# Experts with more than 64 rows: passes of 128 rows on the full array in place of passes of 64 rows, with one turn of the semaphores per expert

## The reference, cut to what matters

```python
hg = jnp.einsum('td,edf->tef', h, w_gate)      # h: 384 tokens x 1024
hu = jnp.einsum('td,edf->tef', h, w_up)        # w_gate, w_up: 16 x 1024 x 512
act = jax.nn.silu(hg) * hu * gates[..., None]
return jnp.einsum('tef,efd->td', act, w_down)  # w_down: 16 x 512 x 1024
```

## Time and profile before

| | |
|---|---|
| median of 3 runs | 616.38 us (616.27 to 617.57) |
| profiled execution | 621.26 us, span 619.4 us |
| PE busy | 492.6 us (80% of the span) |
| DVE, ACT, POOL busy | 224.1, 142.8, 86.1 us |
| bytes moved by DMA | 164.52 MB, mean 266 GB/s |
| `gate_up` instructions on PE (L676) | 672, 165.2 us |
| `down` instructions on PE (L689) | 336, 75.8 us |

### The profile page before, as it was taken

The page is one execution under the profiler, slowest core; times in us unless marked ns, Lnnn a source line. Parts: engine busy times, 40 slices in busy tenths (PEclk is TensorE's granted clock), DMA queues, the critical chain, the costliest instruction groups (busy, mean ns, idle before and its releaser), DMA issues.

```text
span 619.4 us, 7520 instructions
## 1 busy us (share of the span) xinstructions
PE 492.6 (80%) x2624; PEld 234.0 (38%) x2625; DVE 224.1 (36%) x616; ACT 142.8 (23%) x263; POOL 86.1 (14%) x177
## 2 busy tenths in 40 slices
PE   1769889999989999950479899999988878788800
PEld 1225688544478544630243233333332222222200
DVE  3589855999982105560020010110110010101027
ACT  3555842601148201300030010110110010100023
POOL 2000603888000151013000000000000000000030
PEclk9998989999989999975589999999998797978965
DMA  8980340733994931049648993879999999996162
GB/s 296 366 329 0 120 136 6 286 136 120 388 387 183 378 147 43 26 159 392 263 168 335 391 379 108 353 301 411 431 424 423 423 423 422 423 423 266 35 215 107
DMA packets 38032, 164.52 MB, mean 266 GB/s; under 512 B 2776, under 2 KB 3544, under 8 KB 32240
## 3 DMA queue, kind: packets, MB, share of 16 engines
q1 hardware_dynamic: 31120, 145.79, 59.9%
q10 hardware_dynamic: 4608, 10.86, 4.8%
q0 software_dynamic: 2272, 7.46, 3.4%
HBM read 152.76 MB, written 11.34 MB: 265 GB/s over the span
## 4 chain that ended last, share of the span: by engine, by line
issue 51%; PE 30%; DVE 7%; DMA 5%; ACT 4%; POOL 1%; ACTq 0%; POOLq 0%; DVEq 0%
PE psum L604 7%; PE psum L487 3%; PE psum L553 3%; PE psum L479 3%; DMA arena<-in_x_sample 3%; PE psum L509 3%; PE psum L578 3%; PE psum L418 2%; DMA arena<-in_w_mod 2%; PE psum L598 2%; PE psum L628 1%; ACT arena L802 1%; POOL sorted_tokens L1519 1%; DMA arena<-sorted_outputs,pos_u 1%; PE psum L496 1%
## 5 line engine op out<-in xcount | busy, mean ns | idle before, releaser
L676 PE MATMUL psum<-arena 128*64 128x512 f32 x672 | 165.2, 648 | 31.5 <-DMA arena<-in_w_up 21.2
L676 PEld LDWEIGHTS psum<-arena 128*64 128x64 f32 x672 | 51.9, 148 | 131.2 <-issue 111.6
L689 PE MATMUL psum<-arena 128*64 128x512 f32 x336 | 75.8, 592 | 2.3 <-ACTq L972 2.3
L1364 DVE TENSOR_TENSOR arena<-arena,psum 128x256 f32<-128x256 f32 x21 | 8.9, 422 | 183.4 <-ACT arena L956 183.4
L1527 POOL DMA_INDIRECT arena<-sorted_outputs,pos_u x6 | 5.7, 952 | 308.6 <-DMA sorted_outputs<-arena 307.1
L689 PEld LDWEIGHTS psum<-arena 128*64 128x64 f32 x336 | 25.1, 137 | 48.8 <-issue 48.8
L956 ACT ACTIVATE arena<-psum 128x256 f32<-128x256 f32 x21 | 8.1, 384 | 146.2 <-PE psum L676 130.7
L604 PE MATMUL psum<-arena 128*128 128x512 f32 x96 | 41.5, 592 | 0.0
L418 PE MATMUL psum<-arena 128*2 128x256 f32 x256 | 30.7, 395 | 0.3 <-DMA arena<-in_w_mod 0.3
L660 PE MATMUL psum<-arena 128*128 128x128 f32 x48 | 6.7, 302 | 27.0 <-DMA arena<-sorted_tokens 27.0
L961 ACT ACTIVATE arena<-psum 128x512 f32<-128x512 f32 x21 | 12.5, 597 | 66.7 <-PE psum L689 66.7
(11 more groups left out here) (278 smaller groups left out, 586.2 us busy)
## 6 DMA issues: line engine op xcount, KB each, us to landing
arena<-in_w_gate SPq DMA_DIRECT2D x16, 2048.0 KB, 17.5
arena<-in_w_up SPq DMA_DIRECT2D x16, 2048.0 KB, 22.3
arena<-in_w_down SPq DMA_DIRECT2D x16, 2048.0 KB, 19.8
arena<-in_w_mod SPq DMA_DIRECT2D x12, 2048.0 KB, 13.8
arena<-in_w_in SPq DMA_DIRECT2D x3, 2048.0 KB, 19.1
sorted_outputs<-arena ACTq DMA_DIRECT2D x42, 128.0 KB, 6.5
arena<-in_w_out SPq DMA_DIRECT2D x2, 2048.0 KB, 17.5
arena<-modulation_rows ACTq DMA_DIRECT2D x3, 1024.0 KB, 11.2
```

Source lines behind the costliest of these rows:

```text
L676: last = mm(bank[0][HALF * t:HALF * t + HALF, :], xs[:, k, :], gu[:, :, k, t * 256:t * 256 + 256], start=(k == 0), stop=(k == KD - 1))
L689: last = mm(bank[4][HALF * h:HALF * h + HALF, :], hiddenT[:, s * P + t * HALF:s * P + t * HALF + HALF], dn[:, 2 * t + s, h * 512:h * 512 + ...
```

## The change

- An expert of up to 64 rows is computed as before, in one pass (`gate_up_narrow`, `down_narrow`).
- An expert of more than 64 rows has a first pass of 128 rows on the full array: 16 matmuls of 128 columns by 512 for gate and up, each into a PSUM bank of its own (`gate_up_wide`), four transposes, 8 matmuls for down (`down_wide`). Silu, product and copies are twice as wide, the stores 256 KB each.
- Rows beyond 128 go into one or two extra passes of 128 rows with semaphores of their own (`extra_product`, `extra_scalar`, `extra_vector`). In an extra pass every step waits for the one before, and the next expert's first pass begins behind it with nothing beside it.
- The semaphores of the first pass move once per expert: `gated` and `downed` by 2, the others by 1. `skipped` is gone, and `n` is read again at the head of `first_pass`, behind the waits for `xs` and the weights.
- Buffers move within the arena: `xs` and `hidden` are twice as large, silu writes to `hidden`, two staging buffers of 1024 take the place of three of 512. One block of 128 padding rows instead of two.

With the given counts, experts 0, 3 and 15 take one wide pass each, expert 2 a wide pass and a wide extra pass, and the other twelve one narrow pass each.

```diff
-SORTED = PAIRS + 2 * P
+SORTED = PAIRS + P
 SETS = 3
-PASSES = 6
+PASSES = 3
...
-        xs = view(F + 11264, KD, HALF)
-        hiddenT = view(F + 11776, 256)
-        sg = view(F + 12032, 256)
-        hidden = view(F + 12288, 256)
-        ystage = view(F + 12544, 3, 512)
+        xs = view(F + 10240, KD, P)
+        hidden = view(F + 11264, 512)
+        hiddenT = view(F + 11776, 512)
+        ystage = view(F + 12288, 2, D)
...
-        def turn(p, e):
-            return e * PASSES + p
+        def extra(e, q, step, steps):
+            return e * (2 * steps) + (q * steps + step)
+        def all_written(e, q):
+            return e * (32 * PASSES) + (32 * q + 32)
...
-                sp.wait_ge(S("gated"), (e - 2) * PASSES)
+                sp.wait_ge(S("gated"), 2 * (e - 2))
                 load_gate_up(j, e)
-                sp.wait_ge(S("downed"), (e - 2) * PASSES + 1)
+                sp.wait_ge(S("downed"), 2 * (e - 2))
...
+            def gate_up_wide(j, sem):
                 gu = expert_weights(j)[0]
-                pe.wait_ge(S("x_staged"), at + 1)
-                if fresh is not None:
-                    pe.wait_ge(S(f"gu_in{j}"), fresh * 32)
+                for k in range(KD):
+                    for h in range(2):
+                        last = mm(bank[h][:, :], xs[:, k, :], gu[:, h, k, :], start=(k == 0), stop=(k == KD - 1))
+                last.then_inc(S(sem), 1)
+            def gate_up_narrow(j):
+                gu = expert_weights(j)[0]
                 for k in range(KD):
                     for t in range(2):
-                        last = mm(bank[0][HALF * t:HALF * t + HALF, :], xs[:, k, :],
+                        last = mm(bank[0][HALF * t:HALF * t + HALF, :], xs[:, k, 0:HALF],
                                   gu[:, :, k, t * 256:t * 256 + 256], start=(k == 0), stop=(k == KD - 1))
-                last.then_inc(S("gated"), 1)
-            def down(j, fresh, turned, evacuated):
+                last.then_inc(S("gated"), 2)
...
+            def down_wide(j, sem, inc):
                 dn = expert_weights(j)[1]
-                pe.wait_ge(S(f"dn_in{j}"), fresh * 16)
-                pe.wait_ge(S("evacuated"), evacuated + 1)
-                pe.wait_ge(S("turned"), turned + 1)
+                for c in range(4):
+                    for h in range(2):
+                        last = mm(bank[4 + h][:, :], hiddenT[:, c * P:c * P + P], dn[:, c, h * 512:h * 512 + 512],
+                                  start=(c == 0), stop=(c == 3))
+                last.then_inc(S(sem), inc)
...
-            def skipped(e, done):
-                pe.wait_ge(S("gated"), turn(done, e))
-                pe.wait_ge(S("crossed"), turn(done, e))
-                pe.wait_ge(S("downed"), turn(done, e))
-                pe.sem_inc(S("gated"), PASSES - done)
-                pe.sem_inc(S("crossed"), PASSES - done)
-                pe.sem_inc(S("downed"), PASSES - done)
...
+            def first_pass(j, e, fresh, between):
+                pe.wait_ge(S("x_staged"), e + 1)
+                pe.wait_ge(S(f"gu_in{j}"), fresh * 32)
                 n = pe.value_load(n_i[0:1, bass.ds(e, 1)], min_val=0, max_val=NT * P)
                 with pe.If(n > HALF):
-                    gate_up(j, turn(1, e), None)
-                    down(j, use + 1, turn(1, e), turn(0, e))
-                    transposes(turn(1, e))
-                    with pe.If(n > P):
-                        gate_up(j, turn(2, e), None)
-                        down(j, use + 1, turn(2, e), turn(1, e))
-                        transposes(turn(2, e))
-                        with pe.If(n > P + HALF):
-                            with pe.Fori(3, PASSES) as q:
-                                gate_up(j, q + turn(0, e), None)
-                                down(j, use + 1, q + turn(0, e), q + turn(0, e) + -1)
-                                transposes(q + turn(0, e))
-                        with pe.Else():
-                            skipped(e, 3)
+                    gate_up_wide(j, "gated")
+                    between()
+                    pe.wait_ge(S("multiplied"), e + 1)
+                    transposes(4, "crossed")
+                with pe.Else():
+                    gate_up_narrow(j)
+                    between()
+                    pe.wait_ge(S("multiplied"), e + 1)
+                    transposes(2, "crossed")
+            def extra_pass(j, e, q):
+                pe.wait_ge(S("extra_vector"), extra(e, q, 1, 3))
+                gate_up_wide(j, "extra_product")
+                pe.wait_ge(S("extra_vector"), extra(e, q, 2, 3))
+                transposes(4, "extra_product")
+                pe.wait_ge(S("extra_vector"), extra(e, q, 3, 3))
+                if q == 0:
+                    pe.wait_ge(S("evacuated"), e + 2)
+                else:
+                    pe.wait_ge(S("extra_scalar"), extra(e, 0, 2, 2))
+                down_wide(j, "extra_product", 1)
+            def extra_passes(j, e, m):
+                extra_pass(j, e, 0)
+                with pe.If(m > 2 * P):
+                    extra_pass(j, e, 1)
+                with pe.Else():
+                    pe.wait_ge(S("extra_scalar"), extra(e, 0, 2, 2))
+                    pe.sem_inc(S("extra_product"), 3)
+            def expert(j, e, use):
+                nothing = lambda: None
+                m = pe.value_load(n_i[0:1, bass.ds(e, 1)], min_val=0, max_val=NT * P)
+                following = ((j + 1) % SETS, e + 1, use + (j + 1) // SETS + 1)
+                with pe.If(m > HALF):
+                    with pe.If(m > P):
+                        down(j, e, use + 1, True, 1)
+                        extra_passes(j, e, m)
+                        pe.wait_ge(S("extra_product"), extra(e, 2, 0, 3))
+                        pe.sem_inc(S("gated"), 1)
+                        pe.sem_inc(S("downed"), 1)
+                        pe.wait_ge(S("extra_scalar"), extra(e, 2, 0, 2))
+                        first_pass(*following, nothing)
                     with pe.Else():
-                        skipped(e, 2)
+                        pe.sem_inc(S("gated"), 1)
+                        pe.sem_inc(S("extra_product"), 6)
+                        first_pass(*following, lambda: down(j, e, use + 1, True, 2))
...
+                    first_pass(*following, lambda: down(j, e, use + 1, False, 2))
...
+            def extra_pass(e, q, y):
+                row = first_row(e, P * (q + 1))
+                act.wait_ge(S("extra_product"), extra(e, q, 1, 3))
+                A(hidden[:, :], bank[0][:, :], ACT.Silu).then_inc(S("extra_scalar"), 1)
+                act.wait_ge(S("extra_product"), extra(e, q, 3, 3))
+                A(ystage[:, y, :], psum[:, 4:6, :].rearrange("p a b -> p (a b)"), ACT.Copy
+                  ).then_inc(S("extra_scalar"), 1)
+                act.wait_ge(S("extra_scalar"), extra(e, q, 2, 2))
+                act.wait_ge(S("written"), all_written(e, q + 1))
+                store_wide(row + P * (q + 1), y)
+            def extra_passes(e, y, m):
+                extra_pass(e, 0, 1 - y)
+                with act.If(m > 2 * P):
+                    extra_pass(e, 1, y)
+                with act.Else():
+                    act.wait_ge(S("extra_product"), extra(e, 2, 0, 3))
+                    act.sem_inc(S("extra_scalar"), 2)
+                    act.sem_inc(S("written"), 32)
+            def no_extra():
+                act.sem_inc(S("extra_scalar"), 4)
+                act.sem_inc(S("written"), 64)
...
+                with act.If(m > HALF):
+                    with act.If(m > P):
+                        evacuate_wide(e, y)
+                        extra_passes(e, y, m)
+                        act.wait_ge(S("written"), all_written(e, 3))
+                        gate(e + 1)
...
+            def multiply_wide(sem):
+                tt(hidden[:, :], hidden[:, :], bank[1][:, :], ALU.mult).then_inc(S(sem), 1)
...
+            def expert(e):
+                m = dve.value_load(n_i[0:1, bass.ds(e, 1)], min_val=0, max_val=NT * P)
+                nxt = dve.value_load(off_i[0:1, bass.ds(e + 1, 1)], min_val=0, max_val=PAIRS)
+                with dve.If(m > P):
+                    main_turn(e)
+                    extra_passes(e, m)
+                    stage_x(nxt, "x_staged")
+                with dve.Else():
+                    dve.sem_inc(S("extra_vector"), 6)
+                    stage_x(nxt, "x_staged")
+                    main_turn(e)
+                multiply(e + 1)
```

More of the change, by code:

```diff
@@ L711, in expert_rest, with transposes, down @@
-            def expert_rest(j, e, use):
+                last.then_inc(S("downed"), 2)
+            def transposes(n, sem):
+                for c in range(n):
+                    last = tr(bank[2][:, c * P:c * P + P], hidden[:, c * P:c * P + P], ident[:, :])
+                last.then_inc(S(sem), 1)
+            def down(j, e, fresh, wide, inc):
+                pe.wait_ge(S(f"dn_in{j}"), fresh * 16)
+                pe.wait_ge(S("evacuated"), e + 1)
```

(58 more changed lines are left out.)

178 lines of the change are left out of this document (66 added, 112 removed).

## The result

The changed kernel takes 716.5 us (median of four runs, 708.0 to 720.0) against 616.3 us: a ratio of 1.158, interval 1.151 to 1.164. I had forecast 638 us, in a range of 631 to 645. The direction was right and the size was wrong by 78 us.

What follows compares the result with a forecast made beforehand. The prediction took the weight stream, started by expert 3's last `down`, as the bound. A shift of 21.5 us, plus 0.6 for stores, less 0.3 in the tail, gave 21.8 on the median of 616.4: 638.2 us, range 631 to 645.

Steps and rivals of the forecast that it cites:

- the code loading: Rival: PE stops 1.19 us for code at turns of experts 1 to 4 and within the extra pass; 644 us, chance 0.12.
- What bounds the kernel before: The weight stream sets the end, 15.4 us per expert; its start depends on PE finishing expert 3's last `down`.
- the decisive point: End of expert 3's last `down`, 415.9 us before; said to move expert 15's weights one for one.
- the stores: Expert 3's rows stored once, behind the point: 0.26 MB more in the stream, 0.6 us.
- A wide pass costs two narrow ones: On PE, wide `gate_up` 13.8 us against 13.84 for two narrow; wide `down` 6.9 against 2 x 3.46.
- Expert 2's extra 10.3 us: Expert 2 pays two wide passes, 41.4 us, for three narrow ones, 31.1: 10.3 us more ahead of the point.
- The open steps: Extra pass: silu and product exposed before the transposes, 1.4 us, and the copy before `down`, 0.8 us.
- the turn to expert 3: After expert 2's extra pass PE waits for ACT's copies and stores, 3.0 us, plus 0.6 for the row-count load.
- The sum without reloading: PE's steps with no code reloads, through the weight stream and tail to the kernel's end: 638.2 us.
- The forecast shift of 21.5 us: Delay of expert 3's last `down`: 17.5 us from the steps plus 4.0 from slow clock starts.
- The clock: Slow starts after waits: 2.5 us at expert 3's `gate_up`, 1.5 at expert 4's, 4.0 together; bounds 0 and 9.
- The tail: From the arrival of expert 15's weights to the end of the kernel: 0.3 us less than before.

Runs made afterwards that it cites:

- compact: The changed kernel with PE's code for an expert written once, branches choosing only a step's matmuls; loop body 91 KB; 647.3 us, 1.051 to before.
- compact_short_one: compact with a narrow extra pass for at most 64 remaining rows and without PE's code for rows beyond 256; 636.2 us, 1.028 to before.
- pad157: The kernel before with 104 matmuls per expert that never run in the innermost branch; loop body 157 KB; 672.7 us, 1.088 to before.
- noweights: The changed kernel without the weight loads of experts 3 to 15, SP only setting their semaphores; 692.1 us, 1.121 to before.
- pad100: The kernel before with 28 matmuls per expert that never run in the innermost branch; loop body 100 KB; 654.6 us, 1.064 to before.
- nosecond: The changed kernel without PE's code for the second extra pass, which no expert runs; loop body 137 KB; 732.9 us, 1.186 to before.

## Why the prediction was wrong, point by point

**The step that failed** is the code loading. The sum put it at nothing, and the rival, with a chance of 0.12, had its price and its reach wrong: "5 x 1.19 = 6 more: 644. Later turns are covered by the stream." A stop costs not 1.19 but 9.5 to 14.0 us at eight of the turns, with two to six code packets in each; what I took for the price, the 1.19 us at 350.25, came behind one packet at 347.9 and may be only the visible end of its load. And the loads come back on every turn of the loop, up to the last experts, where PE has only 3.7 us to spare against the weights (15.4 less 11.7); so PE becomes the bound and the stream gets holes. Written once, the same steps took 69 us less. The page of before had the number that would have warned: 19 code packets, all of PE's code once. I did not set the 157 KB of the new loop beside the 79 KB of the old one.

**What bounds the kernel before** was right: in compact, which is bound by the weights again, expert 15 starts 29.5 us later where the decisive point moved by 27.8 and the stores were put at 0.6.

**A wide pass costs two narrow ones**: right. 13.9 and 7.1 us were measured, 13.8 and 6.9 forecast.

**Expert 2's extra 10.3 us**: right, 11.1 by the medians of compact and compact_short_one, 10.0 by their traces.

**The open steps**: right. 1.41 and 0.86 us against 1.4 and 0.8; the turn to expert 3 3.92 against 3.6.

**The sum without reloading** was too low as well: 638.2 against the compact form's 647.3, which lies outside my range. The forecast shift of 21.5 us has 0.9 ahead of the first `gate_up`; from its start on it is 20.6, where 27.8 (139.8 less 112.0) were measured. Of the 7.2 us missing, 4.9 lie ahead of expert 1's `gate_up`: from the end of expert 0's product (322.94) to 330.72 are 7.8 us where I had 2.9. The same stretch at expert 4 took 3.5. One code packet falls in this stop, so I take it for a first load of code; that it is one was not tested by itself. Another 1.5 is the first wide `gate_up`, 16.5 us for 15.0, at a granted clock of 0.84. The other terms are off by less than 1 us each.

**The clock**: `gate_up` of expert 3 took 15.69 us for 13.9, 1.8 where I had 2.5; that of expert 4 9.40 for 7.09, 2.3 where I had 1.5. That they give 4.1 against 4.0 together is luck in part, since one was too high and the other too low. Reloading adds to it: PE was busy for 515.0 us in the changed kernel and 502.5 in compact, with the same matmuls, because most of its stops are followed by a slow start.

**The tail**: from the start of expert 15's `gate_up` to the end of the span, 58.6 us in compact and 60.2 before. That is 1.6 less, where I had 0.3 less.

**What stays open**: the rule by which blocks are kept or dropped. The packets by body size are not in order, and pad157 and the changed kernel, with 61 and 63 packets, are 44 us apart. Part of that is the 30 us which the compact form pays without reloads; the rest is not split up. Nor is it known why PE stops for 2.9 to 3.2 us at experts 8, 11 and 14 of the changed kernel, where no code packet falls in the stop and noweights, without weights to wait for, has the same.

## What to carry to other kernels

Count the bytes of the code between a loop's head and its end, branches that never run included (shown here for PE alone), and look at the code queue's packets: as many as the program has blocks means loaded once, more means that the loop doesn't fit. Choose by branch the single step, not a copy of the whole sequence. And before a wider tile is adopted, price it by count over busy time: two narrow matmuls side by side took what one wide one took, so only the rounding up of rows was left to decide, and it went against the wide pass.

## What the runs showed of the hardware that was not expected

- PE's loop bodies of 79, 90 and 91 KB were loaded once (19 to 21 packets in the whole program); bodies of 100 KB and more were reloaded (34 to 66).
- Stops for code at a jump took 9.5 to 14.0 us in the changed kernel, with 2 to 6 packets of 16 KB in each, and 5.0 to 13.9 us without the weights' traffic. Inside a matmul sequence one took 2.4 us in pad100 and 2.75 us in nosecond.
- A stop for code has no releaser in the profile: it stands as "issue" (in the changed kernel, in the row of 95.2 us), or as PE's own queue (PEq, 72.2 us in pad157) at the line of the branch ahead.
- It seems that a register load behind a wait hides what the wait was for. In the compact form PE's waits at experts 9 to 14 stand as "issue", 1.6 to 4.7 us each; before they stood as waits for the up weights, 1.7 to 4.7 us.
